# Issuing the next chunk's input preparation in the middle of the current chunk, in the two projection loops of a hybrid decoder layer

## The chip, the cores and the metric

The program runs on the 8 cores of one Trainium2 chip. Every core runs the same instructions on its own data; nothing is exchanged between cores. The metric is the device time of the slowest core in microseconds (us).

## The reference, cut to what matters

One decoder layer on x of shape (2, 8192, 1024), float32: a norm, two groups of attention heads on the same normalised input, an output projection, and a mixture of 32 experts.

```python
xn = rmsnorm(h, norm_mix[l])
h = h + token_mixer(xn, ...)                      # one w_in for both head groups
hn = rmsnorm(h, norm_ffn[l])
h = h + hierarchical_moe(hn, ...)

# token_mixer
proj = xn @ w_in                                  # 3*512 + 3*512 + 8 columns
qa = rmsnorm(heads(qa), q_norm_fox); ka = rmsnorm(heads(ka), k_norm_fox)
logf = log_sigmoid(fa + b_forget)                 # 8 columns, then a cumulative sum
oa = forgetting_attention(qa, ka, va, logf)       # full causal, 8 heads of 64
qb = rope(rmsnorm(heads(qb), q_norm_dil), pos); kb = rope(rmsnorm(heads(kb), k_norm_dil), pos)
ob = dilated_attention(qb, kb, vb)                # windows up to 2048 back, 8 heads
```

The root mean square of x is not applied to x before the projection. The kernel projects the raw x in bf16, computes the sum of squares beside it, and corrects the projected values.

## The kernel before, in words

A core owns four chunks of 512 tokens of one batch row. The program has five stages; the change touches the first two, called W and A here.

**Stage W** (lines 469 to 553) treats the dilated heads. For each of the four owned chunks (`ti`) it walks five chunks of 512 tokens (`wc`), the owned one last: 20 in all. For every chunk it projects K (four blocks of 128 columns, `hp`) and V (four blocks of 128 tokens), and for `wc == 4` also Q (four blocks). After the fifth chunk comes the attention of that `ti`.

**Stage A** (lines 565 to 687) treats the forgetting heads: 16 chunks with K, V and the 8 forget columns (called f here), and then four chunks with Q alone.

Every chunk begins with `chunk_pre` (line 319): two loads of 1 MB by SP into `xf`, on ScalarE a Copy of `xf` to `xb` (bf16) and a Square of it to `xsq`, on TensorE 8 matmuls of `xsq` with ones (the sum of squares by token) and 32 narrow ones (the same by partition), and on VectorE and ScalarE the small tiles `et`, `rt` and, in A, `r8`. `xf` has two buffers in both stages, `xb` and `xsq` have one in W and two in A.

A K or Q block is a list of stages (`norm_stages`, line 346). s0 is 8 matmuls and a Square on ScalarE (`ksq`). s1 is one matmul on `ksq`, a step on VectorE, Ln and Exp on ScalarE, and a step on VectorE (`kn` in W, `a_kt` in A). s2, in W alone, is one matmul on `kn` (the rotation), then POOL and VectorE. `Pipe` runs a block's stages one push apart: push `hp` issues s2 of block hp-2, s1 of block hp-1 and s0 of block hp, and `vproj(hp)` follows. `drain` issues what is left at a chunk's end, so the last s1 and s2 stand there with no projection between them. In A, `drain` is followed by the f matmuls and a chain on VectorE and ScalarE over the tile `a_fz` (lines 646 to 659), which ends in a cumulative sum; its transposes (`ctok_tr`) are put off into the next chunk's `hp == 2`.

The order of the work is the order in which the Python code runs. Each operation goes to the end of its engine's instruction list, and an engine takes its list strictly in order; semaphores are waited for where a buffer is read or written (`Sched`, line 41). PSUM banks come from small rings: "raw" for K and Q, "h" for s1 and s2, "m" for V, `chunk_pre` and f. In the names of the trace `wxb,Ww` is a K or Q projection of stage W and `Ww,wxb` a V projection; in stage A they are `axb,Wa` and `Wa,axb`.

Of the kernel before, what the change touches and what calls it, by code (L numbers as in the profile page):

```python
# [7 lines left out]
F32 = mybir.dt.float32  # L8
# [7 lines left out]
CH = 512  # L16
NCH = 16
# [151 lines left out]
def build():  # L169
# [5 lines left out]
    xT = din("xT", [NCH, 128, 8, CH])  # L175
    xTw = din("xTw", [4, 5, 128, 8, CH])
# [14 lines left out]
    cosw = din("cosw", [4, 128, 5 * CH])  # L191
    sinw = din("sinw", [4, 128, 5 * CH])
# [6 lines left out]
    with ExitStack() as es:  # L199
        S = Sched(nc, es)  # L200

        def sbt(stack, name, shape, dt):
            return stack.enter_context(nc.sbuf_tensor(name, list(shape), dt))
# [114 lines left out]

        def chunk_pre(P, src_ap, slot, need_r8):
            xf, xb, xsq = P["xf"][slot], P["xb"][slot], P["xsq"][slot]  # L320
            xfB, xbB, xsqB = P["xfB"][slot], P["xbB"][slot], P["xsqB"][slot]
            S.dma("sp", xf[:, 0:4, :], src_ap[:, 0:4, :], (), [xfB], chan="xf%d" % slot)
            S.dma("sp", xf[:, 4:8, :], src_ap[:, 4:8, :], (), [xfB], chan="xf%d" % slot)
            act(xb[:].rearrange("p c t -> p (c t)"), xf[:].rearrange("p c t -> p (c t)"), AF.Copy, [xfB], [xbB])
            act(xsq[:].rearrange("p c t -> p (c t)"), xf[:].rearrange("p c t -> p (c t)"), AF.Square, [xfB], [xsqB])
            bk, bb = nbank()
            for c in range(8):
                mm(bk[:, :], ones_bf, xsq[:, c, :], c == 0, c == 7, [xsqB, P["cB"]], [bb])
            et, etB = P["et"][slot], P["etB"][slot]
            ts("dve", et[:, :], bk[:, :], EPS / 1024.0, ALU.mult, [bb], [etB], s2=EPS * EPS, op1=ALU.add)  # L330
            if need_r8:
                r8, r8B = P["r8"], P["r8B"]
                ts("dve", r8[0:8, :], bk[0:8, :], 1.0 / 1024.0, ALU.mult, [bb], [r8B], s2=EPS, op1=ALU.add)
                act(r8[0:8, :], r8[0:8, :], AF.Ln, [r8B], [r8B])
                act(r8[0:8, :], r8[0:8, :], AF.Exp, [r8B], [r8B], scale=-0.5)
            bk2, bb2 = nbank()
            for t4 in range(4):
                for c in range(8):
                    mm(bk2[:, 2 * t4:2 * t4 + 2], xsq[:, c, t4 * 128:(t4 + 1) * 128], cb[:, 0:2], c == 0, c == 7,
                       [xsqB, P["cB"]], [bb2])  # L340
            rt, rtB = P["rt"][slot], P["rtB"][slot]
            ts("dve", rt[:, 0:8], bk2[:, 0:8], 1.0 / 1024.0, ALU.mult, [bb2], [rtB], s2=EPS, op1=ALU.add)
            act(rt[:, 0:8], rt[:, 0:8], AF.Ln, [rtB], [rtB])
            act(rt[:, 0:8], rt[:, 0:8], AF.Exp, [rtB], [rtB], scale=-0.5)
# [36 lines left out]

            return [s0, s1] if rope is None else [s0, s1, s2]

        def alloc_proj(stack, pre, need_r8, nxb=2):
            P = {}
            P["cB"] = constB[0]
            P["xf"] = [sbt(stack, pre + "xf%d" % i, [128, 8, CH], F32) for i in range(2)]
            xbl = [sbt(stack, pre + "xb%d" % i, [128, 8, CH], BF16) for i in range(nxb)]
            xsl = [sbt(stack, pre + "xsq%d" % i, [128, 8, CH], BF16) for i in range(nxb)]
            P["xb"] = [xbl[0], xbl[-1]]  # L390
            P["xsq"] = [xsl[0], xsl[-1]]
            P["et"] = [sbt(stack, pre + "et%d" % i, [128, CH], F32) for i in range(2)]
            P["rt"] = [sbt(stack, pre + "rt%d" % i, [128, 8], F32) for i in range(2)]
            for nme in ("et", "rt"):
                P[nme + "B"] = [S.buf(pre + nme + "B%d" % i) for i in range(2)]
            P["xfB"] = [S.buf(pre + "xfB%d" % i) for i in range(2)]
            for nme in ("xb", "xsq"):
                bl = [S.buf(pre + nme + "B%d" % i) for i in range(nxb)]
                P[nme + "B"] = [bl[0], bl[-1]]
            if need_r8:  # L400
                P["r8"] = sbt(stack, pre + "r8", [8, CH], F32)
                P["r8B"] = S.buf(pre + "r8B")
            P["nt"] = [(sbt(stack, pre + "ksq%d" % i, [128, CH], BF16), sbt(stack, pre + "t%d" % i, [128, CH], F32),
                        sbt(stack, pre + "t2%d" % i, [128, CH], F32), sbt(stack, pre + "kn%d" % i, [128, CH], BF16))
                       for i in range(3)]
            P["ntB"] = [tuple(S.buf(pre + "ntB%d_%d" % (i, q)) for q in range(4)) for i in range(3)]
            return P
# [59 lines left out]
        cB = constB[0]  # L467
        OtokB[0] = S.buf("Otok")
        with ExitStack() as pw:
            P = alloc_proj(pw, "w", False, nxb=1)  # L470
            stg = sbt(pw, "w_stg", [128, 8, 256], F32)
            stgB = S.buf("stgw")
            Ww = sbt(pw, "Ww", [128, 8, 1536], BF16)
# [16 lines left out]
            scrB = S.buf("wscr")  # L490
            midx = [0, 1, 2, 3] + [4] * 8 + [5, 6, 7, 8, 9] + [9, 9, 9]
            kcount = 0
            for ti in range(4):
                for wc in range(5):
                    slot = (ti * 5 + wc) % 2
                    src = xTw[ti, wc]
                    chunk_pre(P, src, slot, False)
                    xb, xbB = P["xb"][slot], P["xbB"][slot]
                    et, etB = P["et"][slot], P["etB"][slot]
                    rt, rtB = P["rt"][slot], P["rtB"][slot]  # L500
                    S.dma("sp", cs[slot][0][:, :], cosw[ti, :, wc * CH:(wc + 1) * CH], (), [csB[slot]], chan="cs%d" % slot)
                    S.dma("sp", cs[slot][1][:, :], sinw[ti, :, wc * CH:(wc + 1) * CH], (), [csB[slot]], chan="cs%d" % slot)
                    rope = (cs[slot][0][:, :], cs[slot][1][:, :], csB[slot])
                    pipe = Pipe()

                    def vproj(t4, xb=xb, xbB=xbB, rt=rt, rtB=rtB, wc=wc):
                        bk, bb = nbank("m")
                        for c in range(8):
                            mm(bk[:, :], xb[:, c, t4 * 128:(t4 + 1) * 128], Ww[:, c, 1024:1536], c == 0, c == 7, [xbB, WwB], [bb])
                        act(Vw[:, wc * 4 + t4, :].rearrange("p (h e) -> p h e", e=65)[:, :, 0:64],  # L510
                            bk[:, :].rearrange("p (h e) -> p h e", e=64), AF.Copy, [bb, rtB], [VwB],
                            scale=rt[:, 2 * t4:2 * t4 + 1])

                    for hp in range(4):
                        pipe.push(norm_stages(P, Ww, WwB, 512 + hp * 128, xb, xbB, et, etB, g_qk(3), rope,
                                              KTw[:, hp, wc * CH:(wc + 1) * CH], KTwB, kcount))
                        kcount += 1
                        vproj(hp)
                    if wc == 4:
                        for hp in range(4):  # L520
                            pipe.push(norm_stages(P, Ww, WwB, hp * 128, xb, xbB, et, etB, g_qk(2), rope,
                                                  QTd[:, hp, :], QTdB, kcount))
                            kcount += 1
                    pipe.drain()
# [40 lines left out]
        with ExitStack() as pa:  # L565
# [23 lines left out]
            fzB = S.buf("fz")  # L589
            kcount = 0  # L590
            deferred = []
            for kc in range(NCH + 4):
                slot = kc % 2
                is_q = kc >= NCH
                if is_q:
                    while deferred:
                        deferred.pop(0)()
                if not is_q:
                    src = xT[kc]
                else:  # L600
                    ti = kc - NCH
                    src = xTw[ti, 4]
                chunk_pre(P, src, slot, not is_q)
                xb, xbB = P["xb"][slot], P["xbB"][slot]
                et, etB = P["et"][slot], P["etB"][slot]
                rt, rtB = P["rt"][slot], P["rtB"][slot]
# [1 line left out]
                if is_q:  # L608
                    ti = kc - NCH
                    for hp in range(4):  # L610
                        pipe.push(norm_stages(P, Wa, WaB, 1032 + hp * 128, xb, xbB, et, etB, g_qk(0), None,
                                              QTf[:, hp, ti * CH:(ti + 1) * CH], QTfB, kcount))
                        kcount += 1
                    pipe.drain()
                    continue
# [10 lines left out]
                for hp in range(4):  # L626
                    if hp == 2:
                        while deferred:
                            deferred.pop(0)()
                    ks = kcount % 4  # L630

                    def spill(hp=hp, ks=ks, kc=kc):
# [9 lines left out]
                bk, bb = nbank()  # L642
                for c in range(8):
                    mm(bk[0:8, :], Wa[:, c, 1024:1032], xb[:, c, :], c == 0, c == 7, [WaB, xbB], [bb])
                r8, r8B = P["r8"], P["r8B"]
                z, mneg, na = fz[:, 0, :], fz[:, 1, :], fz[:, 2, :]
                tt("dve", z, bk[0:8, :], r8[0:8, :], ALU.mult, [bb, r8B], [fzB])
                ts("dve", z, z, bf_sb[:, 0:1], ALU.add, [fzB, cB], [fzB])
# [447 lines left out]
```

How the kernel before makes its waits and increments, by code:

```python
        def run_engine(ename, h):  # L113
            waited = {}
            for op in per_eng[ename]:
                need = {}
                for i in op.deps:
                    d = ops[i]
                    if d.chan is not None:
                        sem, k = chan_sems[d.chan], ("c", d.chan)
                    else:
                        sem, k = sems[d.eng], ("e", d.eng)
                    if need.get(k, (None, 0))[1] < d.value:
                        need[k] = (sem, d.value)
                for k, (sem, v) in need.items():
                    if waited.get(k, 0) < v:
                        h.wait_ge(sem, v)
                        waited[k] = v
                inst = op.fn(h)
                if op.chan is not None:
                    inst.then_inc(chan_sems[op.chan], 16)
                elif op.signal:
                    inst.then_inc(sems[op.eng], 1)
            last = {}
            for op in per_eng[ename]:
                if op.chan is not None:
                    last[op.chan] = op.value
            for c, v in last.items():
                if waited.get(("c", c), 0) < v:
                    h.wait_ge(chan_sems[c], v)
```

## Time and profile before

| what | us |
|---|---|
| median of 2 runs | 6435.11 |
| the two runs | 6395.51, 6474.72 |
| the profiled execution, slowest core | 6422.19 |
| its span (core 6) | 6420.5 |
| spans of the 8 cores | 6369.4 to 6420.5 |
| busy: PE, DVE, ACT, POOL | 5355.3, 2358.3, 2452.0, 766.0 |

The span is the time from a core's first to its last instruction. "Busy" is the time in which an engine executed something; it is an average over stages with different limits. PE is TensorE, ACT is ScalarE, DVE is VectorE, POOL is GpSimd, SP issues loads. The granted clock of TensorE has in this trace two main levels, written 1.00 (2.4 GHz) and 0.50 (1.2 GHz). All rows are of core 6, the slowest.

### The profile page before, as it was taken

To read this page: it belongs to the slowest core of one execution; us is meant where nothing else is said; L and a number is where in the kernel's file an instruction comes from. 1 tells how busy PE (TensorE), PEld (TensorE's weight loads), DVE (VectorE), ACT (ScalarE), POOL (GpSimd) and SP (SyncE) were. 2 spreads that over 40 slices of the span, in tenths; PEclk is the share of its full clock that TensorE was granted. 3 is DMA by queue.
4 is the path that set the end of the run, shared out by engine and by line. 5 is a ranking of instruction groups with operands and counts; after the bars stand their busy time and mean duration, and the time that the engine had idled before them with its cause. 6 is when DMAs were issued, how large, how long until landed. Compare 5 with 4: busy or idle time off the path is not lost. (4 is left out here: it accounts for less than half of the span.)

```text
span 6420.5 us, 86558 instructions; the slowest of 8 cores (6369.4 to 6420.5 us)
## 1 busy us (share of the span) xinstructions
PE 5355.3 (83%) x27090; PEld 2312.7 (36%) x27090; DVE 2358.3 (37%) x3842; ACT 2452.0 (38%) x3549; POOL 766.0 (12%) x748
## 2 busy tenths in 40 slices
PE   2787878736655799999947799999999999999999
PEld 1333333312222233333315344444444444444444
DVE  1333343423333234333315334333343334433343
ACT  3566666645555577777742011111111111111111
POOL 1212121201110000000002211111110111101110
PEclk9767666658778555555557899999999999999999
DMA  3111111022221200000011421122211222112211
GB/s 114 52 42 42 47 37 47 4 69 95 97 90 61 59 1 28 28 1 1 1 43 40 140 79 52 67 79 79 79 56 63 79 79 79 58 61 79 79 60 53
DMA packets 109547, 372.64 MB, mean 58 GB/s; under 512 B 13616, under 2 KB 32048, under 8 KB 98736
## 3 DMA queue, kind: packets, MB, share of 16 engines
q1 hardware_dynamic: 102960, 350.19, 16.5%
q0 software_dynamic: 6144, 16.92, 0.7%
q8 instruction: 232, 3.80, 0.2%
q14 instruction: 211, 1.73, 0.1%
HBM read 341.76 MB, written 25.30 MB: 57 GB/s over the span
## 5 line engine op out<-in xcount | busy, mean ns | idle before, releaser
L243 PE MATMUL pb<-hnT,oreg 128*128 128x512 bf16 x8192 | 1824.3, 384 | 35.9 <-POOL oreg L271 35.9
L256 ACT ACTIVATE gs<-pb 128x512 bf16<-128x512 f32 x512 | 305.7, 597 | 2533.2 <-PE pb L243 2533.2
L243 PEld LDWEIGHTS pb<-hnT,oreg 128*128 128x128 bf16 x8192 | 809.6, 99 | 1031.3 <-issue 149.9
L243 PE MATMUL pb<-wdb,HT 128*128 128x512 bf16 x4096 | 909.6, 380 | 136.3 <-DVE HT L265 136.3
L256 ACT ACTIVATE pt<-pb,biasT 128x512 bf16<-128x512 f32 x1280 | 876.9, 687 | 252.2 <-PE pb L452 136.5
L265 DVE TENSOR_TENSOR HT<-pb,gs 128x512 bf16<-128x512 f32 x512 | 354.1, 692 | 1467.4 <-PE pb L243 1467.4
L268 DVE SCALAR_TENSOR_TENSOR hsb<-pb,comb,hsb 128x512 f32<-128x512 f32 x1024 | 767.6, 751 | 284.8 <-PE pb L243 264.4
L243 PE MATMUL pb<-QTf,KTp 64*128 64x512 bf16 x1280 | 772.2, 605 | 37.4 <-DMA KTp<-Kd 37.4
L268 DVE SCALAR_TENSOR_TENSOR pt<-fm,tab,pt 128x512 bf16<-128x512 bf16 x512 | 380.9, 751 | 730.6 <-PE pb L452 612.6
L243 PEld LDWEIGHTS pb<-wdb,HT 128*128 128x128 bf16 x4096 | 392.1, 98 | 651.8 <-issue 204.7
L271 POOL CAST oreg<-d_stg 128x1024 bf16<-128x1024 f32 x256 | 264.6, 1040 | 2215.9 <-PE pb L243 2163.5
L452 PE MATMUL pb<-V,pt 128*128 128x65 bf16 x5120 | 516.0, 243 | 14.7 <-DVE pt L268 11.8
L452 PEld LDWEIGHTS pb<-V,pt 128*128 128x128 bf16 x5120 | 309.7, 122 | 572.1 <-issue 572.1
L256 ACT ACTIVATE wpt<-pb,tab 128x512 bf16<-128x512 f32 (+3 forms) x640 | 416.4, 655 | 152.9 <-ACT wpt L256 65.4
L243 PE MATMUL pb<-QTd,KTw 64*128 64x512 bf16 (+3 forms) x640 | 364.8, 574 | 9.4 <-POOL QTd L265 9.4
L265 DVE TENSOR_TENSOR wpt<-wpt,dm 128x512 bf16<-128x512 bf16 (+3 forms) x640 | 253.7, 404 | 250.4 <-ACT wpt L256 214.0
L243 PE MATMUL pb<-axsq,cb 128*128 128x512 bf16 x160 | 69.4, 614 | 324.8 <-ACT axsq L256 324.8
L452 PE MATMUL pb<-Vw,wpt 128*128 128x65 bf16 x2368 | 245.5, 242 | 27.1 <-DVE wpt L265 24.0
L452 PEld LDWEIGHTS pb<-Vw,wpt 128*128 128x128 bf16 x2368 | 144.7, 121 | 286.0 <-issue 284.5
L243 PE MATMUL pb<-wxsq,cb 128*128 128x512 bf16 x160 | 71.4, 626 | 210.6 <-ACT wxsq L256 210.6
L265 POOL TENSOR_TENSOR wt<-wkn,cos 128x512 f32<-128x512 bf16 x96 | 111.4, 1161 | 932.9 <-DVE wkn L268 773.3
L243 PE MATMUL pb<-wxb,Ww 128*128 128x512 bf16 x768 | 194.1, 399 | 0.0
(122 smaller groups left out, 3307.3 us busy)
## 6 DMA issues: line engine op xcount, KB each, us to landing
d_stg<-wg SPq DMA_DIRECT2D x128, 512.0 KB, 8.1
d_stg<-wu SPq DMA_DIRECT2D x128, 512.0 KB, 6.6
d_stg<-wd SPq DMA_DIRECT2D x128, 512.0 KB, 7.4
wxf<-xTw SPq DMA_DIRECT2D x40, 1024.0 KB, 4.9
axf<-xT SPq DMA_DIRECT2D x32, 1024.0 KB, 4.9
Vd<-a_v POOLq DMA_DIRECT2D x64, 130.0 KB, 2.0
V<-Vd SPq DMA_DIRECT2D x16, 520.0 KB, 5.0
Kd<-a_kt POOLq DMA_DIRECT2D x64, 128.0 KB, 2.1
```

The costliest lines, as they stand in the source:

```text
L243: S.op("pe", lambda e: e.matmul(out, lhsT, rhs, start=start, stop=stop), R, W)
L256: S.op("act", lambda e: e.activation(out=out, in_=in_, func=func, **kw), R, W)
L265: S.op(eng, lambda e: e.tensor_tensor(out=out, in0=in0, in1=in1, op=op), R, W)
L268: S.op("dve", lambda e: e.scalar_tensor_tensor(out=out, in0=in0, scalar=scalar, in1=in1, op0=op0, op1=op1), R, W)
L271: S.op(eng, lambda e: e.tensor_copy(out=out, in_=in_), R, W)
L452: S.op("pe", (lambda o, l, r, a, b: (lambda e: e.matmul(o, l, r, start=a, stop=b, skip_group_check=True)))(ob[:, qb * 65:(qb + 1) * 65], p ...
```

## The change

In both loops `chunk_pre` of chunk g+1 is issued inside chunk g, right before the push of block `hp == 2`; in stage A behind the put-off transposes. Only the first chunk's stands ahead of its loop. In W the loads of the two rope tables move with it. The buffers follow: in W `xb` and `xsq` get two buffers and `xf` is cut to one, and in A `r8` gets two. The instructions are the same in number and kind.

```diff
-        def alloc_proj(stack, pre, need_r8, nxb=2):
+        def alloc_proj(stack, pre, need_r8, nxb=2, nxf=2):
...
-            P = alloc_proj(pw, "w", False, nxb=1)
+            P = alloc_proj(pw, "w", False, nxb=2, nxf=1)
...
+            def w_pre(g):
+                ti_, wc_ = g // 5, g % 5
+                sl = g % 2
+                chunk_pre(P, xTw[ti_, wc_], sl, False)
+                S.dma("sp", cs[sl][0][:, :], cosw[ti_, :, wc_ * CH:(wc_ + 1) * CH], (), [csB[sl]], chan="cs%d" % sl)
+                S.dma("sp", cs[sl][1][:, :], sinw[ti_, :, wc_ * CH:(wc_ + 1) * CH], (), [csB[sl]], chan="cs%d" % sl)
+
+            w_pre(0)
             for ti in range(4):
                 for wc in range(5):
-                    slot = (ti * 5 + wc) % 2
-                    src = xTw[ti, wc]
-                    chunk_pre(P, src, slot, False)
+                    g = ti * 5 + wc
+                    slot = g % 2
...
                     for hp in range(4):
+                        if hp == 2 and g + 1 < 20:
+                            w_pre(g + 1)
                         pipe.push(norm_stages(P, Ww, WwB, 512 + hp * 128, xb, xbB, et, etB, g_qk(3), rope,
...
+            def a_pre(kc_):
+                if kc_ < NCH:
+                    chunk_pre(P, xT[kc_], kc_ % 2, True)
+                else:
+                    chunk_pre(P, xTw[kc_ - NCH, 4], kc_ % 2, False)
+
+            a_pre(0)
             for kc in range(NCH + 4):
...
-                chunk_pre(P, src, slot, not is_q)
...
                     for hp in range(4):
+                        if hp == 2 and kc + 1 < NCH + 4:
+                            a_pre(kc + 1)
                         pipe.push(norm_stages(P, Wa, WaB, 1032 + hp * 128, xb, xbB, et, etB, g_qk(0), None,
...
                     if hp == 2:
                         while deferred:
                             deferred.pop(0)()
+                        if kc + 1 < NCH + 4:
+                            a_pre(kc + 1)
```

The first place is TensorE's list in stage W, at the border of two chunks. `wxsq,cb` and `cb,wxsq` are the sum of squares, `wkn,cb` is s2 and `wksq,cb` is s1. Before:

```order
L243 MATMUL pb<-Ww,wxb 128x512 x8
L243 MATMUL pb<-wkn,cb 128x512
L243 MATMUL pb<-wksq,cb 128x512
L243 MATMUL pb<-wkn,cb 128x512
L243 MATMUL pb<-wxsq,cb 128x512 x8
L243 MATMUL pb<-cb,wxsq 128x2 x32
L243 MATMUL pb<-wxb,Ww 128x512 x8
L243 MATMUL pb<-Ww,wxb 128x512 x8
L243 MATMUL pb<-wksq,cb 128x512
L243 MATMUL pb<-wxb,Ww 128x512 x8
L243 MATMUL pb<-Ww,wxb 128x512 x8
L243 MATMUL pb<-wkn,cb 128x512
```

And with the change:

```order
L243 MATMUL pb<-Ww,wxb 128x512 x8
L243 MATMUL pb<-wkn,cb 128x512
L243 MATMUL pb<-wksq,cb 128x512
L243 MATMUL pb<-wkn,cb 128x512
L243 MATMUL pb<-wxb,Ww 128x512 x8
L243 MATMUL pb<-Ww,wxb 128x512 x8
L243 MATMUL pb<-wksq,cb 128x512
L243 MATMUL pb<-wxb,Ww 128x512 x8
L243 MATMUL pb<-Ww,wxb 128x512 x8
L243 MATMUL pb<-wxsq,cb 128x512 x8
L243 MATMUL pb<-cb,wxsq 128x2 x32
L243 MATMUL pb<-wkn,cb 128x512
```

The two rows on `wxsq` went from the border of the chunks to behind the second V projection; now they belong to the chunk after.

The second place is ScalarE's list in stage A, from the last block of a chunk (`at`) on. `a_fz` is the chain behind f, `axb` and `axsq` are Copy and Square of the input, `ar` and `art` the small tiles, `a_v` the eviction of V. Before:

```order
L256 ACTIVATE at<-at 128x512 x2
L256 ACTIVATE a_fz<-a_fz 8x512 x2
L256 ACTIVATE axb<-axf 128x4096
L256 ACTIVATE axsq<-axf 128x4096
L256 ACTIVATE ar<-ar 8x512 x2
L256 ACTIVATE art<-art 128x8 x2
L256 ACTIVATE aksq<-pb 128x512
L256 ACTIVATE a_v<-pb,art 128x4x2x64
L256 ACTIVATE at<-at 128x512 x2
L256 ACTIVATE aksq<-pb 128x512
L256 ACTIVATE a_v<-pb,art 128x4x2x64
```

And with the change:

```order
L256 ACTIVATE at<-at 128x512 x2
L256 ACTIVATE a_fz<-a_fz 8x512 x2
L256 ACTIVATE aksq<-pb 128x512
L256 ACTIVATE a_v<-pb,art 128x4x2x64
L256 ACTIVATE at<-at 128x512 x2
L256 ACTIVATE aksq<-pb 128x512
L256 ACTIVATE a_v<-pb,art 128x4x2x64
L256 ACTIVATE axb<-axf 128x4096
L256 ACTIVATE axsq<-axf 128x4096
L256 ACTIVATE ar<-ar 8x512 x2
L256 ACTIVATE art<-art 128x8 x2
```

Copy and Square went behind the second V eviction; the first `aksq` of a chunk now stands directly behind `a_fz`.

## Rows read from the trace of the kernel before

**Rows 1.** Windows, stages W and A: us, busy and (count) by engine, PEclk, DMA share, GB/s.

```profile
75.00:1360.00 1285.00, 993.23 (x5408) 408.14 (x5408) 486.42 (x1034) 791.58 (x1090) 236.59 (x195) 0.68 0.13 44
1360.00:2101.00 741.00, 391.61 (x2226) 172.48 (x2226) 234.43 (x403) 386.18 (x477) 71.96 (x129) 0.76 0.26 87
```

**Rows 2.** What PE waited for in stage W: us in total, times, longest.

```profile
PE pb L243 <- ACT wxsq L256: 210.6, 20, 99.5
PE pb L243 <- DVE wkn L268: 104.7, 66, 4.0
```

**Rows 3.** What PE waited for in stage A.

```profile
PE pb L243 <- ACT axsq L256: 324.8, 20, 98.1
```

**Rows 4.** Timeline, border of two W chunks: start, us, engine, instruction, [idle before <-releaser].

```profile
435.64 3.60 ACT L256 ACTIVATE wxb<-wxf 128x4096 bf16<-128x4096 f32 x1
...
436.75 0.38 PE L243 MATMUL pb<-wkn,cb 128*128 128x512 bf16 x1 [3.69 <-DVE wkn L268]
...
439.15 3.60 ACT L256 ACTIVATE wxsq<-wxf 128x4096 bf16<-128x4096 f32 x1
...
442.89 3.57 PE L243 MATMUL pb<-wxsq,cb 128*128 128x512 bf16 x8 [5.77 <-ACT wxsq L256]
...
447.15 2.17 PE L243 MATMUL pb<-wxb,Ww 128*128 128x512 bf16 x8
```

**Rows 5.** Timeline, the same chunk's middle: second V, its eviction, first rotation.

```profile
452.84 1.89 PE L243 MATMUL pb<-Ww,wxb 128*128 128x512 bf16 x8
...
454.61 0.38 PE L243 MATMUL pb<-wkn,cb 128*128 128x512 bf16 x1
...
454.82 0.69 ACT L256 ACTIVATE Vw<-pb,wrt 128x512 bf16<-128x512 f32 x1 [0.81 <-PE pb L243]
```

**Rows 6.** Windows over the border of rows 4.

```profile
435.00:437.00 2.00, 0.25 (x1) 0.10 (x1) 0.75 (x1) 1.91 (x3) 0.35 (x2) 1.00 0.00 0
437.00:438.00 1.00, 0.12 (x1) 0.00 (x0) 0.69 (x1) 1.00 (x1) 0.97 (x1) 0.77 0.00 0
...
447.00:448.00 1.00, 1.00 (x14) 0.51 (x12) 0.43 (x2) 0.24 (x2) 0.00 (x0) 0.61 0.30 123
```

**Rows 7.** Timeline of PE, a pause among the Q blocks of a W chunk.

```profile
559.99 0.38 PE L243 MATMUL pb<-wkn,cb 128*128 128x512 bf16 x1 [1.97 <-DVE wkn L268]
...
560.53 3.52 PE L243 MATMUL pb<-wxb,Ww 128*128 128x512 bf16 x8
```

**Rows 8.** Timeline, one A chunk: sum of squares, first K, second V, f, next chunk.

```profile
1683.53 3.49 PE L243 MATMUL pb<-axsq,cb 128*128 128x512 bf16 x8 [12.89 <-ACT axsq L256]
...
1687.66 1.89 PE L243 MATMUL pb<-axb,Wa 128*128 128x512 bf16 x8
...
1693.19 1.89 PE L243 MATMUL pb<-Wa,axb 128*128 128x512 bf16 x8
...
1703.01 1.89 PE L243 MATMUL pb<-axb,Wa 128*8 128x512 bf16 x8
...
1709.28 1.35 ACT L256 ACTIVATE a_fz<-a_fz 8x512 f32<-8x512 f32 x2 [3.96 <-DVE a_fz L265]
...
1717.79 3.43 PE L243 MATMUL pb<-axsq,cb 128*128 128x512 bf16 x8 [12.89 <-ACT axsq L256]
```

**Rows 9.** Window in which the clock came back in that A chunk.

```profile
1686.00:1687.00 1.00, 1.00 (x9) 0.45 (x8) 0.00 (x0) 0.00 (x0) 0.00 (x0) 0.59 0.98 418
```

**Rows 10.** Timeline, two Q chunks of stage A.

```profile
2017.39 3.57 PE L243 MATMUL pb<-axsq,cb 128*128 128x512 bf16 x8 [9.40 <-ACT axsq L256]
...
2044.09 3.57 PE L243 MATMUL pb<-axsq,cb 128*128 128x512 bf16 x8 [9.41 <-ACT axsq L256]
```

**Rows 11.** Tile view of `wxf`: its 40 loads.

```profile
DMA to landing us min/median/max: 4.7/4.9/9.2
```

**Rows 12.** Timeline, last step of an attention in stage W, before the next chunk.

```profile
406.13 0.42 DVE L265 TENSOR_TENSOR oreg<-pb,wrl 128x256 bf16<-128x256 f32 x1
...
412.20 3.57 PE L243 MATMUL pb<-wxsq,cb 128*128 128x512 bf16 x8 [6.46 <-ACT wxsq L256]
```

More of the change, by code:

```diff
@@ L321, in chunk_pre @@
             xfB, xbB, xsqB = P["xfB"][slot], P["xbB"][slot], P["xsqB"][slot]
-            S.dma("sp", xf[:, 0:4, :], src_ap[:, 0:4, :], (), [xfB], chan="xf%d" % slot)
-            S.dma("sp", xf[:, 4:8, :], src_ap[:, 4:8, :], (), [xfB], chan="xf%d" % slot)
+            xch = "xf%d" % (slot % P["nxf"])
+            S.dma("sp", xf[:, 0:4, :], src_ap[:, 0:4, :], (), [xfB], chan=xch)
+            S.dma("sp", xf[:, 4:8, :], src_ap[:, 4:8, :], (), [xfB], chan=xch)
             act(xb[:].rearrange("p c t -> p (c t)"), xf[:].rearrange("p c t -> p (c t)"), AF.Copy, [xfB], [xbB])
@@ L331, in chunk_pre @@
             if need_r8:
-                r8, r8B = P["r8"], P["r8B"]
+                r8, r8B = P["r8"][slot], P["r8B"][slot]
                 ts("dve", r8[0:8, :], bk[0:8, :], 1.0 / 1024.0, ALU.mult, [bb], [r8B], s2=EPS, op1=ALU.add)
@@ L382, in norm_stages @@
             return [s0, s1] if rope is None else [s0, s1, s2]
-        def alloc_proj(stack, pre, need_r8, nxb=2):
+        def alloc_proj(stack, pre, need_r8, nxb=2, nxf=2):
             P = {}
             P["cB"] = constB[0]
-            P["xf"] = [sbt(stack, pre + "xf%d" % i, [128, 8, CH], F32) for i in range(2)]
+            xfl = [sbt(stack, pre + "xf%d" % i, [128, 8, CH], F32) for i in range(nxf)]
+            P["xf"] = [xfl[0], xfl[-1]]
             xbl = [sbt(stack, pre + "xb%d" % i, [128, 8, CH], BF16) for i in range(nxb)]
@@ L395, in alloc_proj @@
                 P[nme + "B"] = [S.buf(pre + nme + "B%d" % i) for i in range(2)]
-            P["xfB"] = [S.buf(pre + "xfB%d" % i) for i in range(2)]
+            xfbl = [S.buf(pre + "xfB%d" % i) for i in range(nxf)]
+            P["xfB"] = [xfbl[0], xfbl[-1]]
+            P["nxf"] = nxf
             for nme in ("xb", "xsq"):
@@ L400, in alloc_proj @@
             if need_r8:
-                P["r8"] = sbt(stack, pre + "r8", [8, CH], F32)
-                P["r8B"] = S.buf(pre + "r8B")
+                P["r8"] = [sbt(stack, pre + "r8%d" % i, [8, CH], F32) for i in range(2)]
+                P["r8B"] = [S.buf(pre + "r8B%d" % i) for i in range(2)]
             P["nt"] = [(sbt(stack, pre + "ksq%d" % i, [128, CH], BF16), sbt(stack, pre + "t%d" % i, [128, CH], F32),
@@ L500, in build @@
                     rt, rtB = P["rt"][slot], P["rtB"][slot]
-                    S.dma("sp", cs[slot][0][:, :], cosw[ti, :, wc * CH:(wc + 1) * CH], (), [csB[slot]], chan="cs%d" % slot)
-                    S.dma("sp", cs[slot][1][:, :], sinw[ti, :, wc * CH:(wc + 1) * CH], (), [csB[slot]], chan="cs%d" % slot)
                     rope = (cs[slot][0][:, :], cs[slot][1][:, :], csB[slot])
@@ L597, in build @@
                         deferred.pop(0)()
[L598 to L602, printed above, removed]
-                chunk_pre(P, src, slot, not is_q)
                 xb, xbB = P["xb"][slot], P["xbB"][slot]
@@ L644, in build @@
                     mm(bk[0:8, :], Wa[:, c, 1024:1032], xb[:, c, :], c == 0, c == 7, [WaB, xbB], [bb])
-                r8, r8B = P["r8"], P["r8B"]
+                r8, r8B = P["r8"][slot], P["r8B"][slot]
                 z, mneg, na = fz[:, 0, :], fz[:, 1, :], fz[:, 2, :]
```

## The prediction

> **What bounds the kernel now.** I read the windows by stage first. In stage W TensorE is busy for 993 of 1285 us, in stage A for 392 of 741, and no other engine is busier [rows 1]. So both stages are TensorE plus what it waits for. The later stages run no changed instruction. Then the waits of TensorE: for the Square of the input it waits 210.6 us in W and 324.8 in A [rows 2, 3]. The longest of each, 99.5 and 98.1, is the start of the stage before any chunk and stays. What the change can touch is 111.1 us in 19 waits in W and 226.7 us in 19 waits in A.
>
> The timeline shows how such a wait is made. In W the last block's s2 waits 3.69 us for its kn. ScalarE needs for the next chunk Copy and Square, and from the start of Copy to the first matmul on `wxsq` pass 442.89 - 435.64 = 7.25 us. Copy had begun already 1.1 us before the last s2, so only 5.77 us of it are bare [rows 4]. In A Copy stands behind the `a_fz` chain, and TensorE stands for 12.89 us between f and the sum of squares [rows 8]. In both stages TensorE then works at the low clock: the granted clock comes back to 1.00 near 447.8, 4.9 us after the restart in W, and near 1686.8, 3.3 us after it in A [rows 6, 9].
>
> **The change, part by part.** The ordered lists decide it. The sum of squares of the next chunk now stands on TensorE directly behind the second V projection, and Copy and Square stand on ScalarE directly behind that V's eviction. TensorE takes its list in order. It can't go on to the third K block before the sum of squares, and that one needs all 7.25 us of ScalarE. The work that was meant to cover them stands behind it in the same list.
>
> *The new wait in W.* The second V starts at 452.84 and the next matmul could follow at 454.61; its eviction starts at 454.82 [rows 5]. About 0.6 us later Copy may start, at 455.42, and 7.25 us behind that the sum of squares, at 462.67. V's last matmul ends at 452.84 + 1.89 = 454.73, so TensorE stands for 7.9 us. 19 x 7.9 = 150 us, where 111.1 went away. At the three borders behind an attention the first K now takes a bank that DVE has yet to read, until 406.55, 0.8 us after the last matmul, which ended at 412.20 - 6.46 = 405.74 [rows 12]: 2 us. **W: 150 - 111 + 2 = +41 us.** The end of a chunk with its wait of 3.69 us is unchanged; what is late next there is the same kn. The first half of a chunk took 454.61 - 447.15 = 7.46 us and is only put ahead.
>
> *Stage A.* I set time 0 where f's matmuls are through: 1703.01 + 1.73 = 1704.74. The next K and V follow at once, until 3.5. Then s1 needs the Square `ksq` on ScalarE, which stands behind `a_fz`, over at 1710.63, that is 5.9. It is ready at 6.4: a new wait of 2.8 us, in the 15 chunks that follow an f. Second K and V end at 10.1. ScalarE is 0.8 us behind, starts Copy at 11.5, and the sum of squares starts at 18.75. Less 0.4 for the transposes that is a wait of 8.2 us. Behind it two Ln/Exp pairs more stand ahead of the next `ksq`: another 0.8 us by the same way of counting. So 16 x (8.2 + 0.8) + 3 x 8.3 + 15 x 2.8 = 211 us, where 226.7 went away. In the Q chunks one of the waits for `ksq` (1.2 us) falls into the pause, 3 times: -4. **A: about -20 us.** In the three periods between Q chunks alone the wait of 9.4 [rows 10] becomes 8.3.
>
> *The clock.* At the border in W the granted clock is still 1.00 up to 437.00 and falls within the next us [rows 6]. TensorE had at that moment only the pause of 3.69 us behind it, since the s2 matmul ran from 436.75 to 437.13. So a pause of 3.7 us is enough. In the Q blocks one of 1.97 us was: the 8 matmuls behind it took 3.52 us in place of 1.89 [rows 7]. Before, that fall fell together with the longer wait and cost one restart. Now the first K of a chunk follows directly and runs at 0.50, and behind the 7.9 us there is a second restart. Half the time at 0.50 is lost in matmuls that follow each other: 3.3 to 4.9 us give 1.7 to 2.4. I take 2.0. In W 19 x 2.0 = **+38 us**, between 0 and 46. In A it comes behind the wait of 2.8 us, and 0.8 of it is hidden because ScalarE is late anyhow: 15 x 1.2 = **+18 us**, between 0 and 36.
>
> The Trainium skill (TensorE: Matmul & The Clock Gate, "HAM oscillation — how this bites in real kernels") counts the same way: the lost time is the throttled time by (1 - 1.2/2.4). Rows 4 agree: 8 matmuls on `wxsq` in 3.4 us at 0.50 against 1.7 at 1.00. But the same page ("What's actually happening") puts the ramp below 1% of a span for modelling; by that my 56 us, 0.9%, would be left out and the sum would be 6443.
>
> *At nothing:* the single `xf` buffer of W. The load for chunk g+2 may start when Square of g+1 is done, in the middle of chunk g, and is wanted a chunk later, some 30 us; it lands in 4.7 to 9.2 us [rows 11]. Without that cover each chunk would pay up to two landings in a row. SP is moved past nothing, its list is the same. The second `r8` and `xb` cost no instruction. The eviction of a W chunk's third V and POOL's rotation come later with their block and are off TensorE's path.
>
> **Sum**: 41 - 20 + 38 + 18 = +77 us on the profiled 6422.2 us, or 6499; I say **6500 us**. The span is 1.7 us shorter than that time, and the median of the runs shown is 12.9 us above it; the two runs stand 79 us apart. A measurement of this kernel can tell about 2% (129 us) from no change, so this is "the same", on the slow side.
>
> **The rivals.**
>
> 1. *The clock does not fall in the short pauses.* Then +41 - 20 = +21, 6443 us. For it: after the wait of 3.69 us the s2 matmul still ran at 1.00. Against: the window right behind it [rows 6]. Chance 0.25.
>
> 2. *Slower by over 2%: the clock stays down for a whole half chunk.* Place: first K to second V, 7.2 us at 1.00, 14.4 at 0.50. If the clock comes back only behind them, W pays 19 x 7.2 = 137 and A, for its second K and V less the hidden 0.8, 15 x 2.7 = 40: 6422 + 41 - 20 + 137 + 40 = 6620 us. It decides from a restart that takes over 7 us. For it: in the Q pause all 8 matmuls ran at 0.50 [rows 7]. Against: the restarts took 3.3 and 4.9 us [rows 6, 9]. Chance 0.08.
>
> 3. *Hidden, as meant.* TensorE finds the sum of squares ready. Then 111 + 227 go and only the wait behind `a_fz` comes, 42: 6422 - 296 = 6126 us. For it: ScalarE is idle for much of both stages (792 of 1285 us busy in W, 386 of 741 in A [rows 1]). Against: it would have to be 7 us ahead of TensorE at the second V, and it can't evict what is not computed [rows 5]. The Trainium skill (Trainium Kernel Development and Optimization, "Best Practices") says to double-buffer so that DMA overlaps compute; by that rule this change would gain. The trace does not bear that out here: none of the 38 waits is for a load. Chance 0.04.
>
> 4. *The change does less than it says*, because Copy waits for its load in W: each middle pause longer by a landing of 4.9, 19 x 4.9 = 93 on top, 6593. For it: the single buffer. Against: the 30 us above. Chance 0.02.
>
> **How the numbers follow.** My forecast has 0.61, the rest as above. The ends of its terms are 6443 (no clock term) and 6443 + 46 + 36 = 6525. The range must also hold how the runs of one kernel scatter, up to 40 us on a side. I set 6430 to 6560; it takes in the first rival and leaves out the others. Faster by over 2% is rival 3, 0.04. Slower by over 2% (above 6564) is rivals 2 and 4: 0.10. Within 2%: 0.86.
>
> **What would show it.** In the waits: TensorE for `wxsq` 19 times near 7.9 us in place of 5.8, and for `axsq` near 8.2 in place of 12.9; a new entry, `aksq` in A, near 2.8 us 15 times. In the timeline: the pause behind the second V and none ahead of the first K. In the windows: in W two stretches at 0.50 by chunk, the first from the first K on. If the middle pause is missing or under 5 us, my reading of the lists is wrong. If there is one stretch at 0.50 by chunk, rival 1 holds.

## The result and the profile after

The changed kernel takes 6694.27 us, the median of 34 runs (6461.03 to 7041.7). The kernel before, in the same sessions, takes 6621.38 us, the median of 32 (6390.97 to 6956.04). In over half of the runs of either kernel one die or both show a lower granted clock, which lifts both medians by some 230 us; the ratio and all that follows leave those runs, or those cores, out. The ratio is **1.0092, 95% interval 1.0056 to 1.0128**. That is slower by 0.6 to 1.3% and less than 2%: no change by the measure used here, and on the slow side, as forecast. The forecast of 6500 us lies 194 us below the median, and its range (6430 to 6560) doesn't hold it. The ratio counts 14 runs of the change, 13 of them at 6461 to 6468 us, and 10 of before, 8 of them at 6391 to 6397 us: between these the difference is some 70 us, or 1.1%.

The run `e1_change` below is the changed kernel once more. Its profiled execution took 6461.19 us (the slowest core's span 6459.5 us, clock 0.808) and all rows of "after" are from it, of core 2 where no other is named. What TensorE waited for in stage W, 75 to 1420 us (us in total, times, longest), beside [rows 2]:

```profile
PE pb L243 <- ACT wxsq L256: 250.3, 20, 99.5
PE pb L243 <- DVE wkn L268: 116.6, 75, 4.0
PE pb L243 <- DVE oreg L265: 2.9, 3, 1.0
```

Without the first, the waits for the Square are 150.8 us in 19, 7.94 each, where before they were 111.1. The wait for `wkn` grew by 12, and the one for `oreg`, at the borders behind an attention, is new. In stage A, 1420 to 2180 us, beside [rows 3]:

```profile
PE pb L243 <- ACT axsq L256: 246.1, 20, 100.0
PE pb L243 <- ACT aksq L256: 67.7, 43, 3.0
```

146.1 us in 19 (7.7 each) stand where 226.7 stood. But `aksq` now has 67.7 us in 43 waits, and before, in 1360 to 2101 us, it had 18.2 in 16:

```profile
PE pb L243 <- ACT aksq L256: 18.2, 16, 1.3
```

The timeline of a W chunk (start, us, engine, instruction, idle before it) shows the new place of the pause, beside [rows 4, 5]:

```profile
441.88 1.89 PE L243 MATMUL pb<-Ww,wxb 128*128 128x512 bf16 x8
...
443.86 0.69 ACT L256 ACTIVATE Vw<-pb,wrt 128x512 bf16<-128x512 f32 x1 [0.76 <-PE pb L243]
444.45 3.61 ACT L256 ACTIVATE wxb<-wxf 128x4096 bf16<-128x4096 f32 x1
447.95 3.60 ACT L256 ACTIVATE wxsq<-wxf 128x4096 bf16<-128x4096 f32 x1
451.70 3.57 PE L243 MATMUL pb<-wxsq,cb 128*128 128x512 bf16 x8 [7.94 <-ACT wxsq L256]
...
469.16 0.59 PE L243 MATMUL pb<-wkn,cb 128*128 128x512 bf16 x1 [3.70 <-DVE wkn L268]
469.54 3.35 PE L243 MATMUL pb<-wxb,Ww 128*128 128x512 bf16 x8
```

V's eviction, Copy and Square follow each other on ScalarE without a gap, and TensorE stands for all of it. At the end of the chunk the wait of 3.70 us for kn is where it was, and the 8 matmuls of the next chunk's first K behind it take 3.35 us in place of 1.89. The windows over that place (us, busy of PE, PEld, DVE, ACT, POOL, granted clock, DMA share, GB/s), beside [rows 6]:

```profile
467.00:468.00 1.00, 0.00 (x0) 0.00 (x0) 0.00 (x0) 0.91 (x2) 0.52 (x1) 1.00 0.00 0
468.00:470.00 2.00, 0.84 (x3) 0.32 (x4) 0.90 (x2) 0.15 (x1) 0.78 (x1) 0.77 0.00 0
470.00:471.00 1.00, 1.00 (x4) 0.42 (x3) 0.55 (x1) 0.00 (x0) 0.69 (x2) 0.50 0.00 0
```

The granted clock is 1.00 in the pause and 0.50 (1.2 of 2.4 GHz) behind it, while TensorE is fully busy. Sum-of-squares matmuls after the 7.94 us pause also take 3.57 us: two slow stretches by chunk where there was one. A chunk of stage A, beside [rows 8]:

```profile
1708.14 3.55 PE L243 MATMUL pb<-axsq,cb 128*128 128x512 bf16 x8 [7.60 <-ACT axsq L256]
...
1720.76 3.72 PE L243 MATMUL pb<-axb,Wa 128*8 128x512 bf16 x16
...
1727.04 1.35 ACT L256 ACTIVATE a_fz<-a_fz 8x512 f32<-8x512 f32 x2 [3.95 <-DVE a_fz L265]
1728.29 0.57 ACT L256 ACTIVATE aksq<-pb 128x512 bf16<-128x512 f32 x1
...
1729.12 0.59 PE L243 MATMUL pb<-aksq,cb 128*128 128x512 bf16 x1 [2.90 <-ACT aksq L256]
1729.50 3.14 PE L243 MATMUL pb<-axb,Wa 128*128 128x512 bf16 x8
...
1742.30 3.54 PE L243 MATMUL pb<-axsq,cb 128*128 128x512 bf16 x8 [7.60 <-ACT axsq L256]
```

From one sum of squares to the next pass 1742.30 - 1708.14 = 34.16 us, before 1717.79 - 1683.53 = 34.26. The wait of 12.89 us became one of 7.60 and one of 2.90 behind the `a_fz` chain. The clock is low behind both: the sum of squares takes 3.5 us, and the K behind the wait of 2.90 us takes 3.14 in place of 1.89, with the granted clock at 0.50:

```profile
1730.00:1731.00 1.00, 1.00 (x4) 0.37 (x3) 0.90 (x3) 0.00 (x0) 0.54 (x1) 0.50 0.00 0
```

By stage, on core 1 of both profiles. Stage W is counted from the first matmul on `wxsq` to the first on `axsq`, before and after (columns as in the windows above):

```profile
101.90:1443.70 1341.80, 987.09 (x5408) 406.60 (x5409) 495.00 (x1060) 805.43 (x1117) 236.95 (x195) 0.67 0.14 45
98.60:1513.10 1414.50, 1009.48 (x5409) 410.49 (x5409) 494.87 (x1060) 805.61 (x1117) 236.84 (x195) 0.68 0.14 44
```

Stage A is counted from there to the first matmul of the later attention:

```profile
1443.70:2131.20 687.50, 392.30 (x2227) 172.96 (x2228) 225.04 (x375) 364.49 (x446) 71.85 (x129) 0.79 0.26 87
1513.10:2199.90 686.80, 422.73 (x2227) 177.87 (x2228) 223.00 (x375) 359.14 (x446) 71.94 (x129) 0.82 0.26 88
```

W is **72.7 us longer**: for the same matmuls TensorE is busy 22 us longer, and it is idle 50 us longer (405 to 355). A is **0.7 us shorter**: TensorE is busy 30 us longer and idle 31 us less (264 to 295).

### The profile page after: what moved, and what is told of

It is laid out like the page before. It is cut to its first block and busy times, and to the rows that moved or that the text cites. A ratio compares the mean times of both kernels' runs of the same rounds, so it can differ in the third digit from the quotient of the medians.

```text
span 6962.0 us, 86118 instructions; the slowest of 8 cores (6608.9 to 6962.0 us)
## 1 busy us (share of the span) xinstructions
PE 5841.4 (84%) x26748; PEld 2428.6 (35%) x27090; DVE 2355.2 (34%) x3842; ACT 2447.0 (35%) x3549; POOL 766.9 (11%) x748
## 5 line engine op out<-in xcount | busy, mean ns | idle before, releaser
L243 PE MATMUL pb<-hnT,oreg 128*128 128x512 bf16 x8026 | 2125.1, 431 | 51.4 <-POOL oreg L271 37.1
L243 PEld LDWEIGHTS pb<-hnT,oreg 128*128 128x128 bf16 x8192 | 882.9, 108 | 1271.1 <-issue 1177.1
L243 PE MATMUL pb<-wdb,HT 128*128 128x512 bf16 x4016 | 1057.8, 427 | 143.3 <-DVE HT L265 136.0
L243 PEld LDWEIGHTS pb<-wdb,HT 128*128 128x128 bf16 x4096 | 427.2, 106 | 774.7 <-issue 699.4
L243 PE MATMUL pb<-axb,Wa 128*128 128x512 bf16 (+1 forms) x751 | 198.9, 413 | 2.2 <-issue 0.9
```

The source lines that it names most:

```text
L243: S.op("pe", lambda e: e.matmul(out, lhsT, rhs, start=start, stop=stop), R, W)
```

## The experiments

The theory, called T or R1: what costs is where the sum of squares stands in TensorE's list. It is ahead of the work that was to cover Copy and Square, so the pause only moves, and the clock falls once more. The rival R2: ScalarE's work for the next chunk delays the current chunk wherever it is put, or the clock would cost the same anyway. Each ratio is to before on the same chip.

**e1_change**, the change itself, no edit.

> The changed kernel itself, for a profile of an undisturbed core. Theory T (moved waits and a second restart of the clock): about +70 to +77 us on the kernel before (ratio 1.011 to 1.012); on TensorE the wait for wxsq near 7.9 us 19 times, for axsq near 8 us 19 times, the wait for aksq in A grown by 20 to 40 us in total, and in W two stretches at a granted clock of 0.50 in each chunk. Rival R (the clock plays no part, waits alone): the same total, but one stretch at 0.50 per chunk, and stage A some 25 us longer than before.

Measured: 1.0136 (1.0119 to 1.0154). This ratio rests on four runs of the change, at 6461, 6476, 6482 and 6487 us. The lowest is 77 us above the lowest of before in that session (6461.19 to 6383.90) and 71 above the middle one of the nine counted (6390.09). The mean span of cores 0 to 3 is 71 us above that in the profile of before (6448.6 to 6377.5), and in the runs of the result the lowest times are 70 apart. So the change costs some 71 us. There are two slow stretches by chunk in W and stage A is not 25 us longer, which speaks against the rival. The wait for `aksq` grew by 49.5 us, more than the 20 to 40 expected.

**e1_w_only**, the change in stage W alone.

```diff
@@ stage A
-            a_pre(0)
             for kc in range(NCH + 4):
+                a_pre(kc)
...
-                        if hp == 2 and kc + 1 < NCH + 4:
-                            a_pre(kc + 1)
```

> The change in stage W alone; stage A as before. T: W carries the loss, 41 us of waits and 38 of clock, so +75 us (between +60 and +85), more than the whole change. R: +41 us of waits alone.

Measured: 1.0119 (1.0102 to 1.0136), +76 us of 6390. **e1_a_only** is the other half: in W one `xb`, and `w_pre(g)` at the start of the chunk.

> The change in stage A alone; stage W as before. T: -20 us of waits and +18 of clock, so about 0 (between -15 and +10). R: +25 to +30, what is left of the total when W costs 41.

Measured: 1.0006 (0.9994 to 1.0018), +4 us. The loss is stage W's, nearly all. In stage A a pause of 12.89 us was swapped for two that are shorter together, and the slower matmuls behind them take back what that gained.

**e1_fill**, the change and 12 matmuls more in the pause of 3.7 us at the end of each W chunk, into a bank that nobody reads.

```diff
-                    pipe.drain()
+                    while pipe.pending:
+                        if len(pipe.pending) == 1 and len(pipe.pending[0]) == 1:
+                            fb, fbB = nbank("m")
+                            for c in range(12):
+                                mm(fb[:, :], ones_bf, xb[:, c % 8, :], ...)
+                        pipe.step()
```

> The change, and in stage W 12 extra matmuls of 512 columns (2.6 us, results read by nobody) put into the wait of 3.7 us ahead of each chunk's last rotation, 20 times. T: the clock does not fall there any more, the first K of the next chunk runs at 1.00, and the kernel is 25 to 38 us faster than the change. R: the extra matmuls are hidden at best: 0 to +10 us on the change.

Measured: 1.0079 (1.0064 to 1.0094). TensorE's timeline on core 1:

```profile
454.72 2.75 PE L243 MATMUL pb<-wxb,cb 128*128 128x512 bf16 x12
458.65 0.38 PE L243 MATMUL pb<-wkn,cb 128*128 128x512 bf16 x1 [1.17 <-DVE wkn L268]
458.87 1.89 PE L243 MATMUL pb<-wxb,Ww 128*128 128x512 bf16 x8
```

The pause is filled but for 1.17 us, the kn comes no sooner, and the K behind it takes 1.89 us in place of 3.35. By the two ratios that is worth 0.57%, or 36 us, but the four runs behind 1.0136 alone lie 25 us apart. The lowest times differ by 26 us (6435.10 to 6461.19), in the mean of the 8 cores the first matmul on `axsq` comes 25 us sooner (1487.0 to 1512.0), and stage W is 29 us shorter in the mean of cores 0 to 5 (1385.8 to 1414.4). So it is 25 to 29 us. Work that does nothing made the kernel faster: the clock's price is real. The pause at a chunk's end has the next chunk's K right behind it 16 times, so it is 1.6 to 1.8 us each, if nothing of it is won at the four starts of an attention. The same 12 matmuls in the kernel before (**e3_before_fill**, on constants) say whether they do anything where a longer wait follows anyway.

> The kernel before, with 12 extra matmuls of 512 columns (on constants, results read by nobody) in stage W's wait of 3.7 us ahead of each chunk's last rotation, as in the filled kernel of the change. Theory T: the clock falls there in the wait of 5.8 us for Copy and Square anyhow, so the short pause cost nothing of its own before: 0 on the kernel before, between -10 and +10. Rival R (extra matmuls in that pause help by themselves, whatever stands behind): -25 to -38, as they gave the change.

Measured: 0.9998 (0.9978 to 1.0018). They don't: cores 0 to 3 have spans of 6365.9 to 6387.6 us, where they had 6369.4 to 6387.3. So it is the second fall by chunk, the one that the change adds, that the filler takes away.

**e2_sums_late**: the loads, Copy and Square stay in the middle, the sums of squares go behind the cover, ahead of the last s2 of the chunk (in A behind the last block and ahead of f).

```diff
                         if hp == 2 and g + 1 < 20:
-                            w_pre(g + 1)
+                            w_load(g + 1)
+                            pre_cast(P, (g + 1) % 2, 0, 8)
...
-                    pipe.drain()
+                    while pipe.pending:
+                        if g + 1 < 20 and len(pipe.pending) == 1 and len(pipe.pending[0]) == 1:
+                            pre_sums(P, (g + 1) % 2, False)
+                        pipe.step()
```

> The change, with TensorE's part of the input preparation (sums of squares and the small tiles) taken from the middle of the chunk to its end: in W ahead of the last rotation, in A behind the last block and ahead of f. Loads, Copy and Square stay in the middle, in one piece each. Theory T (the loss is TensorE's list: the sums stand ahead of work that could cover the 7.25 us): the wait for wxsq and axsq goes to about 0; a smaller one of some 6 us comes in its place, for kn or aksq of the third block, since Ln and Exp stand behind Copy and Square on ScalarE; the sums fill the pause of 3.7 us in W and the second stretch at 0.50 goes. About -100 us on the kernel before (6290, between -60 and -140). Rival R2 (it is ScalarE's 7.25 us in the middle that cost, wherever the sums stand): within 20 us of the change, +50 to +90 on before.

Measured: one run that can be compared, too few for a ratio: 6320.22 us, where before on that chip takes 6387.5 to 6390.1: some 68 us less, and 141 less than the change, where 100 less than before was expected (60 to 140). All 8 cores agree (6294 to 6319 us). R2 in its strict form falls, which had it 50 to 90 us above before. Its waits, 75 to 2120 us (core 0):

```profile
PE pb L243 <- DVE wkn L268: 166.7, 58, 6.4
PE pb L243 <- ACT aksq L256: 130.4, 59, 6.7
PE pb L243 <- ACT wxsq L256: 99.7, 1, 99.7
PE pb L243 <- ACT axsq L256: 98.9, 1, 98.9
```

The 297 us for the Square are gone: one wait is left by stage, its start. But `wkn` and `aksq` have waits of up to 6.7 us and hold 297 us together, where the change has 116.6 + 67.7 = 184. ScalarE does Copy and Square in one go of 7.2 us, and what TensorE needs of it for the third block stands behind. Waits for `art` (31.7 us in 16) and `a_kt` (17.3 in 3) are new besides, and 297 - 113 - 49 = 135 of the 141 us are accounted for. So moving the reader alone won back about half of the 297 us. R2 is wrong in its size and right in that ScalarE's own order matters too.

**e2_pieces**: Copy and Square cut in four, one piece of each behind each V, the load at `hp == 0`. W gets a second `xf`, which the weights' stage shares, and gives up one `xsq`.

```diff
+                        if hp == 0 and g + 1 < 20:
+                            w_load(g + 1)
...
+                        if g + 1 < 20:
+                            pre_cast(P, (g + 1) % 2, 2 * hp, 2 * hp + 2, False)
```

> As the kernel with the late sums, and Copy and Square cut into four pieces each, one of each behind every V block (in W with two xf and one xsq; the weights' stage shares the second xf). T: no wait of 6 us either; ScalarE needs some 4.7 us per block against 4 on TensorE, so it sets the pace. About -240 us on before (6155, between -180 and -280). R2: ScalarE's total work is the same, so no better than the kernel with the late sums.

Measured: 0.9608 (0.9589 to 0.9627), 6138 us, 17 under the figure expected. R2 falls with it. The earlier load and the other buffers of W came in with the pieces; what each is worth by itself was not run.

**e2_pool**: the same, with Copy on GpSimd (one line: `cp("pool", ...)` in the place of `act(..., AF.Copy, ...)`).

> As the kernel in pieces, with Copy on GpSimd (1.04 us for 1024 columns in the trace of before) and Square on ScalarE. T: ScalarE falls to 3.6 us per block and TensorE sets the pace; what is left is the pause at a W chunk's end and the wait behind a_fz in A. About -330 us on before (6065, between -260 and -370). Rival R3 (GpSimd's casts slow VectorE or the rotation): no better than the pieces on ScalarE.

Measured: **0.944 (0.9413 to 0.9468)**, 6030 us: 358 us under before, 28 more than expected, and the best version. R3 falls: the step on `a_kt` takes VectorE 0.75 us as it did before. Its waits in 75 to 2200 us (core 1):

```profile
PE pb L243 <- ACT axsq L256: 125.5, 20, 99.2
PE pb L243 <- ACT wxsq L256: 115.7, 17, 99.2
PE pb L243 <- ACT aksq L256: 48.9, 46, 2.0
PE pb L243 <- DVE wkn L268: 48.2, 80, 3.8
```

Less the two starts of 99.2 the four lines hold 26.3 + 16.5 + 48.9 + 48.2 = 140 us. In the change they hold 150.8 + 116.6 + 146.1 + 67.7 = 481. So 341 us of waiting went, and the time fell by 431, from 6461 to 6030. The rest is the clock: for the same matmuls of W and A, TensorE is busy for 1331 us where it was for 1432 in the change (core 1 of both). The timeline in stage A:

```profile
1401.74 1.05 POOL L271 CAST axb<-axf 128x1024 bf16<-128x1024 f32 x1
1401.82 1.04 ACT L256 ACTIVATE axsq<-axf 128x1024 bf16<-128x1024 f32 x1
...
1406.68 1.89 PE L243 MATMUL pb<-axsq,cb 128*128 128x512 bf16 x8 [1.57 <-ACT axsq L256]
...
1415.27 1.35 ACT L256 ACTIVATE a_fz<-a_fz 8x512 f32<-8x512 f32 x2 [3.48 <-DVE a_fz L265]
...
1417.24 0.38 PE L243 MATMUL pb<-aksq,cb 128*128 128x512 bf16 x1 [1.70 <-ACT aksq L256]
1417.46 1.89 PE L243 MATMUL pb<-axb,Wa 128*128 128x512 bf16 x8
...
1431.13 1.89 PE L243 MATMUL pb<-axsq,cb 128*128 128x512 bf16 x8 [1.46 <-ACT axsq L256]
```

A chunk takes 24.45 us in place of 34.16. The blocks of 8 matmuls behind the pauses of 1.5 to 1.7 us take 1.89 us: the clock doesn't fall behind them.

**e3_mid_pool** asks what the place is worth with GpSimd's help alone: the change, with only the whole Copy moved there; the sums stay in the middle.

> The change, with Copy on GpSimd in one piece; Square stays on ScalarE and the sums stay in the middle. T: the wait in the middle of a chunk is ScalarE's 7.25 us, so it falls by Copy's 3.5 us, to 4.4 in W and 4.1 in A, 38 times; the clock still falls in it. -133 us on the change, about -60 on before (6335). Rival R4 (the wait is set by something else in the input preparation, as its loads): the wait stays near 7.9.

Measured: 0.9909 (0.9881 to 0.9938), lowest 6331.39 us, expected 6335. R4 falls. Its waits in 75 to 2120 us (core 5):

```profile
PE pb L243 <- DVE wkn L268: 107.8, 60, 3.7
...
PE pb L243 <- ACT wxsq L256: 84.2, 19, 4.4
PE pb L243 <- ACT axsq L256: 79.9, 19, 4.7
```

Copy (3.6 us) is out of the way, and each of the 38 waits is 3.5 us shorter. The middle pause is as long as what ScalarE has to do between V and the sum of squares: 3.6 us less work there is 3.5 us less pause. That is the prediction's way of working it out, shown with another length.

**e2_pool_fz** puts the `a_fz` chain from Exp on off, until behind the next chunk's first V, to take away the wait of 1.70 us.

```diff
+                def fz_rest(kc=kc, z=z, mneg=mneg, na=na):
                     act(na, na, AF.Exp, [fzB], [fzB])
                     act(na, na, AF.Ln, [fzB], [fzB], bias=1.0)
...
+                fzrest.append(fz_rest)
```

> As the kernel with Copy on GpSimd, and in A the chain over a_fz from its Exp on issued behind the next chunk's first V. T: the wait of 2.9 us for the first aksq goes, 15 times: 25 to 45 us less than without. If that wait was something else: no difference.

Measured: a miss. Its two runs take 6065.90 and 6069.41 us, the two of `e2_pool` 6029.86 and 6032.07: 36 us slower where 25 to 45 faster was expected. Timeline (core 2):

```profile
1430.09 0.68 DVE L265 TENSOR_TENSOR a_fz<-a_fz 8x512 f32<-8x512 f32 x1 [2.49 <-ACT a_fz L256]
...
1432.65 0.38 PE L246 MATMUL pb<-idf,cc 8*128 8x8 f32 x4 [1.01 <-DVE cmid L271]
...
1435.13 0.38 PE L243 MATMUL pb<-aksq,cb 128*128 128x512 bf16 x1 [2.10 <-ACT aksq L256]
1435.34 3.21 PE L243 MATMUL pb<-axb,Wa 128*128 128x512 bf16 x8
```

VectorE waits 2.49 us for the Exp and Ln of the chain, and the current block's `at` stands behind that in its list; TensorE then waits twice, 1.01 and 2.10 us, and the clock falls behind it: 3.21 us for the 8 matmuls. The period is 27 us. I had looked for what frees ScalarE and not for VectorE's list: a fault of the kind that the change itself makes.

**e3_fz_split** cuts the chain, ScalarE's part behind the first V, VectorE's behind the second, the transposes at `hp == 3`.

> As the kernel with pieces and Copy on GpSimd, and the chain over a_fz cut in two: its Exp and Ln on ScalarE behind the next chunk's first V, its VectorE part behind the second, the transposes at hp == 3. T: the put-off chain lost because VectorE waited in it for ScalarE and TensorE waited for its result; cut, neither waits, and the wait of 1.7 us for the first aksq is gone too: 15 to 35 us faster than with the chain where it was (6030), 50 to 70 faster than put off whole. If not: no better than 6030.

Measured: 0.9497 (0.9469 to 0.9524) from two runs, 6062.05 and 6075.45 us; again a miss, expected 5995 to 6015. TensorE's timeline on core 6:

```profile
1420.92 0.38 PE L243 MATMUL pb<-aksq,cb 128*128 128x512 bf16 x1 [1.16 <-ACT aksq L256]
...
1425.58 0.38 PE L246 MATMUL pb<-idf,cc 8*128 8x8 f32 x4 [0.84 <-DVE cmid L271]
...
1428.27 2.63 PE L243 MATMUL pb<-axb,Wa 128*128 128x512 bf16 x8 [2.31 <-ACT aksq L256]
```

In this chunk one wait of 1.70 us became three of 1.16, 0.84 and 2.31, and the 8 matmuls took 2.63. In the chunk ahead of it there were two, of 1.22 and 1.29 us, and the matmuls took 1.89. Why the last wait comes in one chunk and not in the other stays open; of the three versions run, the chain costs least where `e2_pool` has it.

## Why the prediction was right in its mechanism and wrong in its time

**What bounds the stages.** Right: all changed time is TensorE's waiting and its clock in W and A. The later stages didn't change.

**The new wait in W**: 7.9 us forecast from V's eviction, Copy and Square, 7.94 measured in 19. Waits for the Square +39.7 (forecast +39), at the attention borders 2.9 for 2. The waits for `wkn` grew by 12 against [rows 2], by 8 against the run with W unchanged (108.3 on core 2): not in the sum. In all W idles 50 us more, 41 forecast.

**Stage A**: forecast was 156 us for `axsq` and 51 for the new `aksq`; measured 146.1 and 49.5. So the waits changed by -31, forecast -20. The wait behind `a_fz` was 2.90, forecast 2.8.

**The clock.** The first rival had it that the clock doesn't fall in the short pause. It does; the filler shows it. The price in W was mis-sized, 38 us for 19 restarts of 2.0. The filler finds 1.6 to 1.8 us each, in the 16 chunks that follow directly. At the three borders behind an attention the first K is slow too (3.57 us at 434.69), but there the clock is at 0.50 from the attention on, which the filler doesn't reach. Over all of W TensorE is busy only 22 us longer: among the Q blocks the clock fell twice in each `ti` before and once in the change (core 2 of both), which the prediction hadn't seen coming. In A TensorE is busy 30 us longer, 18 forecast. The K behind the pause of 2.9 us takes 3.01 to 3.20 us, 15 times (core 2), which is 19 us more than at 1.89; no run filled that pause, and where the other 11 us arise is not shown.

That a pause of 1.97 us is enough, as the prediction read from [rows 7], holds only at times. In the change there are four such pauses in a row among the Q blocks, of 1.91, 1.97, 2.04 and 1.92 us (605 to 619 us). Behind the first three the clock stayed at 1.00, and the K took 1.89 us; behind the fourth it fell. So the length of the last pause alone doesn't decide. The prediction's "3.4 us at 0.50 against 1.7 at 1.00" goes from the first start to the start of what follows; the rows print 3.57 and 1.89, up to the last end.

The rule cited from the Trainium skill (TensorE: Matmul & The Clock Gate, "What's actually happening"), to leave the ramp out of a model since it is under 1% of a span, would have given 6443. Here all slower matmuls together, 22 + 30 us, are 0.8% of the span and so under that 1%, but of the change's effect of 71 us they are over two thirds, since the restarts come back with each chunk.

**The load and the single `xf`**: at nothing, as said. No wait for a load of `wxf` or `axf` between chunks shows in the change.

**The sum**: +77 forecast, some +71 measured. By its terms: waits 50 - 31 = +19, forecast +21; clock 22 + 30 = +52, forecast +56. Each of the four terms was off by 9 to 16 us, and they cancel in pairs. So the mechanism held, and that the sum came within 6 us is in part luck.

**The step that failed** is "The range must also hold how the runs of one kernel scatter, up to 40 us on a side", and with it the base to which the sum was added. I had two times, 79 us apart, and took half of that for the scatter. The 32 runs of before reach from 6391 to 6956, with the middle at 6621: 199 us above the base of 6422.2, and that of the change is 134 us above the end of the range. At the same time the profiled 6422.2 us was high for its own kernel. For the same instructions in the later stages, first the kernel before (core 6), then the run with A alone changed (core 1; window, us, busy by engine):

```profile
2150.00:6410.00 4260.00, 3950.80 (x19356) 1724.59 (x19354) 1610.58 (x2361) 1247.87 (x1940) 448.17 (x418) 0.84 0.17 55
```

```profile
2150.00:6380.00 4230.00, 3919.19 (x19385) 1715.21 (x19383) 1614.01 (x2367) 1254.67 (x1949) 448.17 (x418) 0.84 0.16 56
```

Within 30 matmuls it is the same work, and TensorE is busy 31.6 us longer in the first. In that profile cores 0 to 5 have spans of 6369 to 6387 us, and cores 6 and 7 of 6420.5 and 6413.7. On a base of 6391, the lowest time, the sum gives 6468; 13 of the 14 runs of the change that the ratio counts lie at 6461 to 6468. A range that was meant to hold a median of many runs had to reach as far as times that two runs could not show. The 79 us between them, and cores 6 and 7 at a clock of 0.797 where the others had 0.801 to 0.803, were the sign, and I read it as noise of a fixed size.

**The rivals.** The fully hidden one (6126) did not come. `e2_pieces`, which puts the work where that rival wanted it, takes 6138, but that is near by chance: it still has waits, and it wins back slow matmuls, which the rival left out. `e2_pool` lies 96 us below the rival's figure. That the clock stays down for half a chunk didn't happen: the first V behind a slow K takes 1.89 to 3.14 us, and the second K 1.89 in each of the 19 chunks of W (core 2). Nor did Copy wait for its load: the 19 middle pauses in W are 7.94 us each.

## What to carry to other kernels

Moving a computation earlier hides it only if its consumer, in the list of the engine that takes it in order, stands behind the work that is to cover it. Ask of each moved step on which engine its result is read and what stands behind that reader, and cut what is moved into pieces no longer than the gaps of the engine that does it. With the sum behind the cover, the pieces and the idle GpSimd this same idea is worth 5.6% and not -1%. Before a forecast is added to a measured time, look at the spans and clocks of all cores in that run, and leave room for what few runs can't show.

## What the runs showed of the hardware

- Behind a pause of TensorE of 3.6 to 3.8 us the granted clock was 0.50 in all 16 W chunks of the change that follow directly (the first K takes 2.71 to 3.62 us in place of 1.89, core 2).
- Shorter pauses do it at times. Behind the one of 2.9 us in A the K takes 3.01 to 3.20 us, 15 times. In `e2_pool_fz` it takes 3.21 us behind one of 1.01 and one of 2.10 us, with 0.4 us of work between them. Of four pauses of 1.91 to 2.04 us in a row in the change, the clock fell behind the last alone; behind those of 1.46 to 1.70 us in stage A of `e2_pool` it did not (1.89).
- 12 matmuls of 2.75 us that nobody reads, put in that pause of 3.70 us, made the kernel 25 to 29 us faster; in the kernel before, where a wait of 5.8 us follows anyway, nothing.
- GpSimd makes the bf16 copy of 128x4096 f32 in 3.60 us, as ScalarE does, and that of 128x1024 in 1.05, with ScalarE's Square of the same tile beside it at its usual 1.04 us.
